# Fourteen groups of context value rows summed in the placing stage, and the first query weights fetched a stage ahead

## What is computed

```python
q = (x @ w_q).reshape(N, PEER_HEADS, 2, PEER_D_HALF)
s = einsum('nhpd,pkd->nhpk', q, sub_keys)
s_top, i_top = top_k(s, 16)                       # per head and half
best, best_pos = top_k(sums of all pairs, 16)
expert = idx1 * N_KEYS + idx2                     # 8 heads x 16 = 128 experts per token
g = softmax(best)
act = gelu(einsum('cd,ced->ce', x_c, u[e_c]))     # one row of u per (token, expert)
out = einsum('ce,ced->cd', g_c * act, v[e_c])     # one row of v per (token, expert)
```

## Time and profile before

| | us |
|---|---|
| median of 3 runs | 3699.97 |
| the profiled execution | 3702.06 |
| its span in the profile | 3699.9 |
| PE busy | 3148.5 (85%) |
| DVE busy | 2637.2 (71%) |
| POOL busy | 1974.6 (53%) |
| ACT busy | 1051.0 (28%) |

### The profile page before, as it was taken

One profiled execution on the slowest core, in us unless ns is written; L12 is line 12 of the kernel. 1 busy time (PEld: TensorE's weight loads), 2 busy tenths in 40 slices (PEclk: granted clock), 3 DMA queues, 4 the chain that ended last, 5 costly groups with the idle time before them and its releaser, 6 DMA issues. The chain is left out here.

```text
span 3699.9 us, 47455 instructions
## 1 busy us (share of the span) xinstructions
PE 3148.5 (85%) x15281; PEld 2080.9 (56%) x15281; DVE 2637.2 (71%) x5949; ACT 1051.0 (28%) x1821; POOL 1974.6 (53%) x1776
## 2 busy tenths in 40 slices
PE   6875999698959998476578899998999999999995
PEld 4654446465433333366356566766766666766663
DVE  2328687796557778999677787877877787876346
ACT  4631244464110011376112222222222222222112
POOL 0002555354238885221476677776777677775443
PEclk9887999899979999688789999999999999999997
DMA  9342877667569995286999999999999999999996
GB/s 330 138 143 70 278 255 228 196 229 254 193 236 327 326 316 180 97 246 199 374 382 348 365 406 408 403 385 399 408 403 409 378 406 403 409 407 378 356 342 241
DMA packets 411751, 1133.01 MB, mean 306 GB/s; under 512 B 34088, under 2 KB 129576, under 8 KB 411488
## 3 DMA queue, kind: packets, MB, share of 16 engines
q0 software_dynamic: 221184, 805.40, 58.4%
q1 hardware_dynamic: 174544, 317.82, 23.7%
q10 hardware_dynamic: 15888, 8.13, 0.7%
HBM read 1077.51 MB, written 53.71 MB: 306 GB/s over the span
## 5 line engine op out<-in xcount | busy, mean ns | idle before, releaser
L2295 POOL DMA_INDIRECT exp_value_row<-in_v_rows,exp_v_id x568 | 713.6, 1256 | 279.5 <-issue 176.8
L2342 DVE CUSTOM_DVE_ANT_0 edge_row<-edge_row,edge_x 128x1024 f32<-128x1024 f32 x480 | 584.3, 1219 | 292.5 <-DMA edge_row<-in_u_rows,edge_u_id 257.5
L2287 POOL DMA_INDIRECT edge_row<-in_u_rows,edge_u_id x480 | 507.2, 1057 | 339.3 <-DVE edge_dot L2342 192.4
L379 POOL DMA_INDIRECT ahead_row<-in_u_rows,keep_expert_id x256 | 330.2, 1290 | 354.0 <-DVE keep_dot L389 292.7
L2176 PE MATMUL exp_a_ps<-exp_xT_hi,exp_u_hi 128*128 128x512 f32 x1024 | 410.7, 401 | 20.6 <-DVE exp_u_lo L2311 11.5
L2191 PE MATMUL exp_o_ps<-exp_v_hi,exp_w_hi 128*128 128x512 f32 x1024 | 338.2, 412 | 84.2 <-DVE keep_acc L2406 84.1
L2176 PE MATMUL exp_a_ps<-exp_xT_lo,exp_u_hi 128*128 128x512 f32 x1024 | 402.3, 393 | 0.0
L2176 PE MATMUL exp_a_ps<-exp_xT_hi,exp_u_lo 128*128 128x512 f32 x1024 | 401.5, 392 | 0.0
L2406 DVE TENSOR_TENSOR keep_acc<-exp_o_ps,keep_acc 128x1024 f32<-128x1024 f32 x256 | 312.0, 1221 | 116.0 <-PE exp_o_ps L2191 115.2
L389 DVE CUSTOM_DVE_ANT_0 ahead_row<-ahead_row,ahead_x 128x1024 f32<-128x1024 f32 x256 | 304.4, 1222 | 78.8 <-DMA ahead_row<-in_u_rows,keep_expert_id 75.1
L2162 PE MATMUL exp_v_ps<-exp_value_row,exp_hot 128*32 128x512 f32 x2272 | 280.5, 606 | 60.9 <-DMA exp_value_row<-in_v_rows,exp_v_id 60.9
(11 more groups left out here) (382 smaller groups left out, 5133.9 us busy)
## 6 DMA issues: line engine op xcount, KB each, us to landing
edge_u_raw<-in_uT SPq DMA_DIRECT2D x130, 512.0 KB, 7.1
exp_v_raw<-in_v_rows SPq DMA_DIRECT2D x128, 512.0 KB, 6.7
exp_g_raw<-scratch_g SPq DMA_DIRECT2D x128, 256.0 KB, 6.8
scratch_g<-place_grid SPq DMA_DIRECT2D x3, 8192.0 KB, 35.8
proj_ctx_mod_slab<-in_w_mod SPq DMA_DIRECT2D x8, 2048.0 KB, 15.1
heads_early_room<-in_w_in SPq DMA_DIRECT2D x10, 1024.0 KB, 10.4
exp_value_row<-in_v_rows,exp_v_id POOLq DMA_INDIRECT x568, 8.0
mod_slab<-in_w_mod SPq DMA_DIRECT2D x4, 2048.0 KB, 20.2
```

The costliest lines, as they stand in the source:

```text
L379: nc.gpsimd.indirect_dma_start(out=ahead.row[:, n % KEY_RING, :], out_offset=None, in_=io["u_rows"], in_offset=bass.IndirectOffsetOnAxis(a ...
L2287: nc.gpsimd.indirect_dma_start(out=key_row[:, j % RING, :], out_offset=None, in_=io["u_rows"], in_offset=bass.IndirectOffsetOnAxis(ap=u_id ...
L2295: nc.gpsimd.indirect_dma_start(out=value_row[:, 4 * (j % 2) + t, :], out_offset=None, in_=io["v_rows"].rearrange("a b n -> (a b) n"), in_o ...
L2342: nc.vector.tensor_tensor_reduce(out=key_row[:, j % RING, :], in0=key_row[:, j % RING, :], in1=x, scale=1.0, scalar=0.0, op0=ALU.mult, op1 ...
```

## The change

1. **Placing sums the late groups.** `VALUE_PAIRS` = 3 buffers of two rows are used: two in `keep["acc"]`, one in `edge.u_raw`. POOL gathers a pair of rows (half a group) three steps ahead; in each of the steps 0 to 27 PE does `pair_products` in front of batch 2: 4 matmuls of 128x32 by 512 columns, of two of the four column tiles. ACT builds the stationary columns (`factor_column`, two small copies every second step). After step 27 ACT loads `h2T` into `acc`, copies the sums out and stores them; after step 29 it loads the first two `u_raw`. SP did these loads at the start of the stage.
2. **Experts lose them**: no value gathers, hot columns, value matmuls or `finish(-1)` in the keys rounds.
3. **Query weights**: `Queries.load` puts `w_q`'s first two slabs and `keysT` behind the gate's store on SP in `out_projection`; `routing` waits for them there. To make room the queries `qT` use `ahead.x`, and the third value buffer of the routing stage is `ahead.row`.

```diff
-            for n in KEYS:
+            def gather_pair(p):
+                if p >= VALUE_PAIRS:
+                    pool.wait_ge(values_done, p - VALUE_PAIRS + 1)
+                for j in range(2):
+                    at = (CONTEXT_GATHER - 1) * SLOTS + 4 * GROUPS[p // 2] + 2 * (p % 2) + j
+                    nc.gpsimd.indirect_dma_start(
+                        out=pair[p % VALUE_PAIRS][:, j, :], out_offset=None,
+                        in_=io["v_rows"].rearrange("a b n -> (a b) n"),
+                        in_offset=bass.IndirectOffsetOnAxis(ap=keep["value_id"][:, at:at + 1], axis=0))\
+                      .then_inc(edge.pair_in[p % VALUE_PAIRS], 16)
+            nc.gpsimd.memset(factor_col[:, :, :, :], 0.0).then_inc(columns_zeroed, 1)
+            for n in KEYS[0:KEY_RING]:
                 gather_keys(nc, io, ahead, pool, n)
+            pool.wait_ge(mine_ready, DENSE_TILES)
+            for p in range(VALUE_PAIRS):
+                gather_pair(p)
+            def body(t, m, before):
+                if before + VALUE_PAIRS < PAIRS:
+                    gather_pair(before + VALUE_PAIRS)
+                for n in KEYS[KEY_RING + before:KEY_RING + before + 1]:
+                    gather_keys(nc, io, ahead, pool, n)
...
+            def pair_products(p):
+                g = p // 2
+                pe.wait_ge(column_ready, g + 1)
+                pe.wait_ge(edge.pair_in[p % VALUE_PAIRS], 32 * (p // VALUE_PAIRS) + 32)
+                for j in range(2):
+                    t = 2 * (p % 2) + j
+                    for half in range(2):
+                        last = nc.tensor.matmul(
+                            v_ps[QUAD * t:QUAD * (t + 1), half * SLAB:(half + 1) * SLAB], factor_col[:, g % 2, t, :],
+                            pair[p % VALUE_PAIRS][:, j, half * SLAB:(half + 1) * SLAB],
+                            start=(g == 0), stop=(g == LATE_GROUPS - 1), tile_position=(0, QUAD * t))
+                last.then_inc(values_done, 1)
             def body(t, m, before):
                 for b in range(BATCHES):
+                    if b == 2 and before < PAIRS:
+                        pair_products(before)
...
+            def late_values(before):
+                if before % 2 == 0 and before // 2 + 1 < LATE_GROUPS:
+                    factor_column(before // 2 + 1)
+                if before == PAIRS:
+                    act.wait_ge(values_done, PAIRS)
+                    nc.scalar.dma_start(keep["acc"]..., scratch["h2T"]).then_inc(edge.h2_in, 16)
+                    nc.scalar.activation(out, v_ps[:, :], ACT.Copy).then_inc(late_ready, 1)
+                    act.wait_ge(late_ready, 1)
+                    for t in range(4):
+                        nc.scalar.dma_start(scratch["ffn"][CTX.first + 1][rows, :], out[rows, :]).then_inc(late_stored, 16)
+                if before == PAIRS + 2:
+                    act.wait_ge(late_stored, 64)
+                    for n in range(2):
+                        nc.scalar.dma_start(edge.u_raw[:, n, :, :], io["uT"][n]).then_inc(edge.u_in[n], 16)
...
-            if mode in ("keys", "both") and at_least(r, 1):
-                return [2 * r - 2 + i for i in range(2)]
+            if mode == "both":
+                return [2 * r - 2 * FIRST + i for i in range(2)]
...
-            finish(-1)
```

More of the change, by code:

```diff
@@ L367, in __init__ @@
         self.h2_in = signals.sem("edge_h2_in")
+        self.pair = [self.u_raw[:, :, :, :].rearrange("p e k n -> p e (k n)")]
+        self.pair_in = [signals.sem(f"edge_pair_in{n}") for n in range(VALUE_PAIRS)]
         self.u_in = [signals.sem(f"edge_u_in{n}") for n in range(2)]
@@ L401, with __init__ @@
     GROUPS = P // 4
-    def __init__(self, scope, signals, out):
-        self.row = scope.sb("row", [P, 4 * VALUE_GROUPS, D])
+    def __init__(self, scope, signals, out, last_row):
+        first_rows = scope.sb("row", [P, 4 * (VALUE_GROUPS - 1), D])
+        self.rows = [first_rows[:, 4 * n:4 * n + 4, :] for n in range(VALUE_GROUPS - 1)] + [last_row]
         self.act = scope.sb("act", [P, SLOTS])
@@ L1395, in _, with __init__, load, routing @@
             dots(len(dots_left))
-def routing(nc, io, keep, g, h2T, scratch, routes, ahead=None, val=None, early=None):
+class Queries:
+    def __init__(self, scope, signals):
+        self.slab = scope.sb("slab", [P, 2, KD, SLAB])
+        self.keysT = scope.sb("keysT", [P, 2, N_KEYS])
+        self.slab_in = [signals.sem(f"queries_slab_in{n}") for n in range(2)]
+        self.keys_in = signals.sem("queries_keys_in")
+    def load(self, io, sp):
+        for n in range(2):
+            sp.dma_start(self.slab[:, n, :, :], io["w_q"].rearrange("(j p) n -> p j n", p=P)[:, :, n * SLAB:(n + 1) * SLAB])\
+              .then_inc(self.slab_in[n], 16)
+        sp.dma_start(self.keysT[:, :, :], io["keysT"]).then_inc(self.keys_in, 16)
+def routing(nc, io, keep, g, h2T, scratch, routes, ahead=None, val=None, early=None, queries=None):
     first, second, weight = routes
@@ L1826, in place_weights @@
         KEYS = range(CONTEXT_GATHER * SLOTS, CONTEXT_GATHER * SLOTS + PLACE_DOTS)
+        factorT = s.sb("factorT", [P, P])
+        factor_col = keep["dot"][:, 0:2 * P].rearrange("p (i t n) -> p i t n", i=2, t=4)
+        pair = [keep["acc"][:, 2 * n:2 * n + 2, :] for n in range(2)] + edge.pair
+        out = edge.pair[0][:, 0, :]
+        GROUPS = range(P // 4 - LATE_GROUPS, P // 4)
+        PAIRS = 2 * LATE_GROUPS
         ps = [s.psum(f"ps{n}", [P, SLAB]) for n in range(BATCHES)]
+        v_ps = s.psum("v_ps", [P, D])
         mine_ready = s.sem("mine_ready")
@@ L1938, in _ @@
             sp.dma_start(ahead.x[:, 0, :], scratch["h2"][0]).then_inc(edge.x_in, 16)
-            for n in range(2):
-                sp.dma_start(edge.u_raw[:, n, :, :], io["uT"][n]).then_inc(edge.u_in[n], 16)
-            sp.wait_ge(turned, DENSE_TILES)
-            sp.dma_start(keep["acc"][:, :, :].rearrange("p t n -> p (t n)").rearrange("p (k n) -> p k n", k=KD),
-                         scratch["h2T"]).then_inc(edge.h2_in, 16)
             place = scratch["g"].rearrange("b a t -> a b t")
@@ L2079, in value_groups @@
         def value_groups(r, mode):
-            if mode in ("keys", "both") and at_least(r, 1):
-                return [2 * r - 2 + i for i in range(2)]
+            if mode == "both":
+                return [2 * r - 2 * FIRST + i for i in range(2)]
             if mode == "values":
-                return [4 * r - (4 * LAST - (LATENT_GATHER - 1) * GROUPS) + LATE_GROUPS + i for i in range(4)]
+                return [4 * r - (4 * LAST - (LATENT_GATHER - 1) * GROUPS) + i for i in range(4)]
             return []
         def value_turns(r, mode):
-            if mode in ("keys", "both") and at_least(r, 1):
-                return [r - 1, r - 1]
+            if mode == "both":
+                return [r - FIRST, r - FIRST]
             if mode == "values":
-                start = ((LATENT_GATHER - 1) * GROUPS + LATE_GROUPS) // 2 - 2 * LAST
+                start = ((LATENT_GATHER - 1) * GROUPS) // 2 - 2 * LAST
                 return [2 * r + start + i // 2 for i in range(4)]
@@ L2124, in finish @@
             def finish(k):
-                sp.wait_ge(out_ready, k + 3)
-                if isinstance(k, int) and k < 0:
-                    for t in range(4):
-                        rows = slice(QUAD * (t + 1) - LATE_GROUPS, QUAD * (t + 1))
-                        sp.dma_start(scratch["ffn"][CTX.first + 1][rows, :], out[rows, :]).then_inc(late_stored, 16)
-                else:
-                    sp.dma_start(scratch["ffn"][k + DENSE_TILES], out[:, :]).then_inc(out_stored, 16)
+                sp.wait_ge(out_ready, k + 2)
+                sp.dma_start(scratch["ffn"][k + DENSE_TILES], out[:, :]).then_inc(out_stored, 16)
             walk(sp, body, finish)
@@ L2146, in body @@
                     pe.wait_ge(factor_ready, k + 1)
-                    pe.wait_ge(out_ready, k + 2)
+                    pe.wait_ge(out_ready, k + 1)
                     nc.tensor.transpose(v_ps[:, 0:P], factor[:, :], keep["ident"][:, :]).then_inc(factor_turned, 1)
-                late_tile = mode == "keys" and isinstance(r, int) and r == 1
-                if late_tile:
-                    nc.tensor.transpose(v_ps[:, 0:P], keep["share"][:, SLOTS:2 * SLOTS], keep["ident"][:, :])\
-                      .then_inc(factor_turned, 1)
-                first = tile is not None or late_tile
+                first = tile is not None
                 def values(count):
```

94 lines of the change are left out of this document (62 added, 32 removed).

## The result

| | before | changed |
|---|---|---|
| median | 3700.16 us (6 runs) | 3723.64 us (6 runs) |
| lowest, highest | 3696.9, 3706.17 | 3716.55, 3739.3 |
| ratio | | 1.0070, 95% interval 1.0056 to 1.0084 |
| profiled execution, its span | 3702.06, 3699.9 | 3716.55, 3714.7 |

The changed kernel is slower by 23.5 us between the medians (26 by the ratio), and the forecast was 3722.

A forecast was written before the change was run, and what follows sets the result against it. Placing was taken as bound by a ring through PE and ACT, keys rounds by DVE's work and waits, both rounds as full. Placing +68, experts -41 and query weights -5.5 gave +21.5, hence 3722 us, range 3684 to 3756.

The forecast's parts named there:

- Placing: Placing stage: pairs in PE's stretch lengthen each step to 8.9 us from 6.82; with other edits +68 us (+50 to +85).
- The pair at a whole group's price: Placing step: a pair's 8 records take a 16-record group's full 1.87 us; bounds 0.94 and 3.67.
- Mode switches: Placing: switching between full-width and column-tiled matmuls costs next to nothing; at about 0.1 us each, 3 to 6 us more.
- The clock's toll: Placing: PE's falls to the low clock keep costing 1.13 us a step, since the 1.85 us wait remains.
- the ring: Placing step: scale batch 0 on ACT, PE's four batches, ACT's last copy; 5.69 us at full clock.
- The grid's store fits: Placing: gathers and grid store take 70 us at most within eight steps' 71, so ACT's wait costs 0; otherwise up to 10.
- Experts: Keys rounds: seven rounds at 31.0 us (-30), no token wait (-10), first round -1; together -41 us (-5 to -70).
- Rival 2: Keys rounds: transfers were all that bound them, rounds fall to 27.0 us, -70 instead of -41; 3693 us; chance 0.12.
- Rival 3: Keys rounds: barely gain, the wait being latency already; rounds 34.7 us, -15 instead of -41; 3748 us; chance 0.10.
- Query weights: Routing's start: with the slabs there PE starts some 0.5 us after the stage does, -5.5 us (0 to -7).
- 1: Placing: pair costs 0.94 by record count, half the clock toll, steps of 7.4 us; 3680 us; chance 0.13.
- 4: Placing: the pair is serial or meets the low clock, 3.67 us, +50 more; 3772 us; chance 0.08.

The follow-up runs named there:

- run 2: Changed kernel with matmuls for the first late group only, all gathers, waits and copies kept; ratio to the kernel before 0.9952.
- run 9: Changed kernel with only the pair moved behind the step's last batch, column copies left ahead of ACT's scaling; ratio to the kernel before 0.9961.
- run 3: Changed kernel with a whole group of late products every second step instead of a pair in each; ratio to the kernel before 0.9981.
- run 5: The changed kernel again, unaltered; ratio to the kernel before 1.0072.
- run 10: Changed kernel with only ACT's column copies moved behind its scaling, the pair left in the middle; ratio to the kernel before 1.0089.
- run 1: Changed kernel with the pair behind the step's last batch and the column copies behind ACT's scaling; ratio to the kernel before 0.9946.
- run 8: As run 1, with POOL's gathers begun earlier, a pair's and a key's in turn; ratio to the kernel before 0.9931, 3679.0 us.
- run 11: Run 8 again, unaltered, as the measure for run 12; ratio to the kernel before 0.9943, 3724.8 us.
- run 6: Kernel before with only the early fetch of the query weights; ratio to the kernel before 0.9975.
- run 7: Kernel before with the late sums' four stores issued by ACT behind its copies instead of by SP; ratio to the kernel before 0.9989.
- run 12: Run 11 with each store of the grid sent in two halves of 64 tokens; ratio to the kernel before 0.9914, 3707.6 us.
- the second group: Runs 5 to 8, measured beside a kernel before of 3700.0 us; ratios to it 1.0072, 0.9975, 0.9989 and 0.9931.
- the first and third group: Runs 1 to 4 and 9 to 12, beside kernels before of 3733.4 and 3739.6 us; ratios to them 0.9914 to 1.0116.

## Why the prediction was right

**Placing, +68 predicted, +65.2 measured.** The mechanism is as it was told: the pair stands in PE's stretch, the hole behind it stays at 1.85 to 2.04 us, and the step grows by the pair. Runs 2 and 9 show it from both sides: products gone, the old steps nearly return; products moved past the last batch, the steps fall to DVE's 6.67. By terms:
- *The pair at a whole group's price, 1.87.* Measured 1.92, and runs 3 and 5 show 16 records (1.94) as long as 8.
- *Mode switches.* A full-clock step without late copies is 1.98 + 1.85 + 2.05 + 1.85 = 7.73 us by starts; 5.69 and the pair's 1.92 leave 0.12 for the switch there and back, or 0.19 if the pair is taken from its start to the next batch's (1.85). Run 10 has the same 7.73 with no copies ahead of the scaling. The Trainium skill's drain at a change of tiling mode (TensorEngine Tiling (Array Packing), Key Properties) therefore costs no more than 0.1 us a switch here, 3 to 5 us over the stage.
- *Column copies, 0.2 a step.* The wait rises from 1.85 to 2.04 in every second step only: 0.1 a step. Without them in front (run 10) the stage is 4 to 7 us shorter, 3 of which are the scatter of two equal kernels.
- *The clock's toll, 1.13 a step kept.* The falls remained; 8.74 less the mean full-clock step of 7.83 leaves 0.9. That it is near is partly luck, for the 1.13 was no measure of a toll. It is what the mean step of before (6.82) lies above the ring at full clock, and DVE, which the prediction left out since its work is not in the ring, makes a step in 6.67: it was busy 209.9 of the 211.6 us (run 9). So before the change the low clock cost at most 0.15 a step. It costs in full now that the ring with its pair, 7.83, is longer than DVE's step.
- *First pair +4.* It cost more: the step is 17.07 us, 8.3 above the mean one, 5.38 of them waiting and 1.7 for a pair at the low clock (3.63). Run 5 has 3.71 of wait.
- *Step 28, +3.5*: its wait is 5.49 where 1.85 was, 3.6. *Step 30, +2.5*: PE's wait there is 2.27 instead of 1.85, 0.4; ACT's issues took 0.85 us, not the 2.60 that SP's had.
- *The grid's store fits.* It did, by far: it landed in 45.9 us where I had allowed 70. But this is because steps are long: where eight of them take 53 to 55 us, in runs 1 to 3, 8, 9 and 11, ACT waits 5 to 10 us for the store.

**Experts, -41 predicted, -38.8 measured** (-33.6 between runs 5 and 6). A keys round takes 31.3 us against 31.0 predicted and 35.27 before. The wait for key rows fell by 2.4 a round, where I had taken 3.6; the waits for PE and ACT by 1.0 where I had kept both. Rival 2 (down to 27.0) fails: DVE's own work in a round is still 25.6 us, and 2.9 of the wait for PE stay. Rival 3 (34.7) fails since the rows do come sooner. That the eight gathers gone from a round are what brought them sooner is read from this trace; no run takes them out alone. The 10 us wait for the tokens is gone, and run 7 shows its cause.

**Query weights, -5.5 predicted, -9.0 in the trace, -9 (4 to 15) in run 6.** I took the 6 us between SP's issue and PE's start for the whole of the load's delay. PE's wait itself shrank by 7.3 us, from 22.97 to 15.63: SP's issue (1064.43) comes 1.2 us behind the first instruction of the stage on ACT (1063.22), and with the slabs there PE starts with ACT (1061.40 beside 1061.36) and not 0.5 us later. The other 1.7 us lie ahead of that wait, where the traces with the fetch scatter by 8 us (run 6).

**Rivals.** 1 falls by the pair's price (1.92, not 0.94) and by the step (8.74, over the 8.13 at which it decides). 4 falls by the same rows: the tiles do overlap, and a pair that meets the low clock wholly (3.63) is the first; the others have it in part or not at all (2.63 and 1.92 in the rows above). The total of the late sums is +36 us by the ratios of runs 5 and 6, above my +27; their traces show 29 of it in placing (+63.0) and the experts (-33.6), and 6 before placing starts, in the scatter of the routing stage. The fetch gives 7 to 9 rather than 5.5. Errors of both signs nearly cancel, and the interval of the ratio spans 21 to 31 us over the kernel before: that 3722 came within 2 us of 3724 is luck. That the kernel became slower by some 20 us, and by which stages, is not.

**What the prediction didn't say.** It named the hole in PE and that a matmul in the middle doesn't fill it, and stopped there: it didn't ask what the same pair costs behind the last batch. In the step it costs nothing there (6.67 us beside a mean of 6.82 before), since DVE takes longer than the ring does. Nor did it ask whether DVE, with its 6.67 of 6.82 us, sets the length of a step.

## What to carry to other kernels

In such a ring an engine's idle stretch is filled from behind its last product on which the others wait: the same work ahead of that product is paid in full, here 50 us between two places in a step of 7 us. The work is free only as long as another engine, here DVE with 6.67 us a step, is the slower one, so work out each engine's own time for a step before the ring's. Once the step is short, look for the transfer that had been timed by the long one; here it was the grid's store.

## What was not expected of the hardware

- **With the hole filled the clock stays up, but the same hole doesn't always bring it down.** Before, the granted clock is 0.83 on average in placing, with PE waiting 1.85 us in each step. With the pair in that hole (run 9) it is 1.00 (2.4 GHz) in 1560 to 1620 us. Yet run 3 keeps the hole and has 1.00 for 68.3 us on end, with PE busy 48.85 us where the kernel before has 49.79 and 0.82. What makes the clock fall in one and not in the other stays open. Little of it reaches the time there, since DVE is busy all but 1 or 2% of these stretches. Over the stage, run 12 does the same grid matmuls and 28 pairs in 213.9 us, where the kernel before takes 211.6 for the grid alone.
- **Half a group costs a whole one.** 8 records on two column tiles take 1.92 us, 16 on four 1.94.
- **A store in short runs holds up the queue that issues it.** In run 12 SP's six issues took 388 to 29849 ns, median 17182, those of run 11 372 to 389:

```profile
L2057 SPq DMA_DIRECT2D scratch_g<-place_grid x6: 388/17182/29849, 1547.1 to 1681.0; - x6
```

In order they took 0.39, 6.96, 13.74, 20.62, 27.10 and 29.85 us: they begin 27 us apart and end 33 to 34 apart, the last 30. Nothing stood behind them on SP there but the next store. Each of these stores has as many runs as a whole one (128 in each partition), at half the length; why its issue is held back stays open.
- **Open as well**: the length of what follows. From the end of the keys rounds (the first `exp_factor` of the both rounds) to the end, the traces of the second group and the first two take 1636 to 1654 us, those of the first and third group 1668 to 1699, in code that no run alters; there the kernel before is longer too, by its 3733 and 3740 us. Within a group it is the kernels that get there sooner that take longer (run 9, there at 2029.6: 1693.9 us; run 10, there at 2079.0: 1676.1), so a profile gives back part of what placing gained, while the medians of the same two kernels are 46.8 us apart, as their placing stages are (46.1). The ratios of runs 4 and 10, 1.0116 and 1.0089 where 1.007 would follow from their stages, lie in this scatter. No run was made to tell its cause.
